# One encoder layer on one core: the read of y placed ahead of the stores, output weights split by ScalarE and VectorE, first weights of two groups side by side

## What is computed

```python
h = x @ w_in                                   # 7 parts of 512 columns: u_a, v_a, z_a, q, k, v_b, z_b
a_out = gelu(u_a) * (tril(w_s) @ layernorm(gelu(v_a)) + b_s)     # chunks of 128 frames, 4 channel groups
p = softmax(q @ k.T * HEAD_DIM_B ** -0.5 + bias)                 # own chunk of 64 frames and 8 before it, 8 heads
y = concat(a_out * silu(z_a), (p @ v_b) * silu(z_b))
out = layernorm(ALPHA * x + y @ w_out)
```

## Time and profile before

| | |
|---|---|
| median of three runs | 1073.99 us (1073.51 to 1074.5) |
| the profiled execution | 1073.99 us, of which the span is 1071.9 |
| busy: TensorE, weight loads | 1053.1 us (98%), 912.6 us (85%) |
| busy: VectorE, ScalarE, GpSimd | 459.8, 353.0, 157.2 us |
| chain that ended last | TensorE 97% |
| TensorE's clock over the span | 0.994 of full |

### The profile page before, as it was taken

One profiled execution on the slowest core, in us unless ns is written; L12 is line 12 of the kernel. 1 busy time (PEld: TensorE's weight loads), 2 busy tenths in 40 slices (PEclk: granted clock), 3 DMA queues, 4 the chain that ended last, 5 costly groups with the idle time before them and its releaser, 6 DMA issues.

```text
span 1071.9 us, 17673 instructions
## 1 busy us (share of the span) xinstructions
PE 1053.1 (98%) x7338; PEld 912.6 (85%) x7338; DVE 459.8 (43%) x944; ACT 353.0 (33%) x722; POOL 157.2 (15%) x160
## 2 busy tenths in 40 slices
PE   9999999999999999999999999999999999999995
PEld 7988889999999999999999887777888888888884
DVE  6545442212122111112112001877777777667654
ACT  6410011111111111111112112455666666666620
POOL 0011112020110000000000000742222222322211
PEclk9999999999999999999999999999999999999998
DMA  9561113222211233333331433765444543344112
GB/s 340 199 184 44 45 40 122 80 79 72 74 61 51 103 120 130 118 130 113 118 111 69 122 124 96 261 207 159 137 135 155 157 136 121 109 128 141 58 70 68
DMA packets 112287, 128.43 MB, mean 120 GB/s; under 512 B 7224, under 2 KB 86224, under 8 KB 112208
## 3 DMA queue, kind: packets, MB, share of 16 engines
q1 hardware_dynamic: 107312, 112.62, 32.6%
q10 hardware_dynamic: 4896, 14.68, 4.3%
HBM read 82.17 MB, written 48.26 MB: 122 GB/s over the span
## 4 chain that ended last, share of the span: by engine, by line
PE 97%; DVE 1%; DMA 1%; issue 0%; POOL 0%; POOLq 0%; ACT 0%; DVEq 0%; ACTq 0%; SPq 0%
PE s_ps L1228 35%; PE s_ps L1245 17%; PE out_ps L1430 16%; PE pt_ps L1228 8%; PE o_ps L1394 6%; PE s_ps L1323 6%; PE pt_ps L1365 3%; PE s_ps L1352 1%; PE s_ps L1430 1%; PE o_ps L1257 1%; PE out_ps L1257 1%; PE o_ps L1408 0%; PE out_ps L1264 0%; PE s_ps L1272 0%; DMA yr<-s_y 0%
## 5 line engine op out<-in xcount | busy, mean ns | idle before, releaser
L1228 PE MATMUL s_ps<-xh,ring 128*128 128x512 f32 (+1 forms) x1200 | 341.2, 362 | 0.8 <-ACT st L834 0.8
L1228 PEld LDWEIGHTS s_ps<-xh,ring 128*128 128x128 f32 x1200 | 221.2, 188 | 24.5 <-issue 1.2
L1228 PE MATMUL s_ps<-xl,ring 128*128 128x512 f32 (+1 forms) x600 | 217.1, 362 | 0.0
L1245 PE MATMUL s_ps<-ring,xh 128*128 128x512 f32 x544 | 169.8, 393 | 0.0
L1228 PEld LDWEIGHTS s_ps<-xl,ring 128*128 128x128 f32 x600 | 112.6, 188 | 11.9
L1245 PEld LDWEIGHTS s_ps<-ring,xh 128*128 128x128 f32 x544 | 100.5, 188 | 20.5 <-issue 0.3
L873 ACT ACTIVATE prob<-prob,low 128x640 f32<-128x640 f32 (+3 forms) x128 | 97.6, 764 | 57.5 <-DVE low L1078 57.5
L1078 DVE CUSTOM_DVE_ANT_1 prob<-s_ps,bias 128x640 f32<-128x640 f32 (+1 forms) x112 | 85.7, 803 | 54.5 <-PE s_ps L1323 54.3
L1430 PE MATMUL out_ps<-wo_h,yh 128*128 128x512 f32 x248 | 101.4, 409 | 4.8 <-DVE yl L1180 4.8
L1245 PE MATMUL s_ps<-ring,xl 128*128 128x512 f32 x272 | 106.0, 390 | 0.0
L1430 PE MATMUL out_ps<-wo_l,yh 128*128 128x512 f32 x248 | 98.3, 396 | 0.0
(11 more groups left out here) (151 smaller groups left out, 1225.1 us busy)
## 6 DMA issues: line engine op xcount, KB each, us to landing
raw<-w_all ACTq DMA_DIRECT2D x26, 512.0 KB, 3.6
r<-x SPq DMA_DIRECT2D x17, 512.0 KB, 3.8
q<-s_q SPq DMA_DIRECT2D x16, 512.0 KB, 4.2
k<-s_k SPq DMA_DIRECT2D x16, 512.0 KB, 6.0
y_out<-r SPq DMA_DIRECT2D x15, 512.0 KB, 2.7
x_raw<-x_t SPq DMA_DIRECT2D x12, 384.0 KB, 12.7
s_mix<-st SPq DMA_DIRECT2D x17, 256.0 KB, 2.3
v_all<-st SPq DMA_DIRECT2D x17, 256.0 KB, 2.0
```

The source lines that it names most:

```text
L1228: last = nc.tensor.matmul(bank[b][:, 0:width], w[:, kc, :], xx[:, kc, :], start=kc == 0 and a == 0, stop=kc == KC - 1 and a == 2)
L1245: last = nc.tensor.matmul(out, xx[:, kc, cols], ring[:, 0:GRP, side, kc, :], start=kc == 0 and a == 0, stop=kc == KC - 1 and a == 2)
```

## The change

It has three parts.

```diff
-PIECES = [(0, k0, k0 + 1) for k0 in range(KC)] + [(c, k0, k0 + 2) for c in range(1, NCH) for k0 in range(0, KC, 2)]
+PIECES = [(0, 0, 1, 0, 256), (0, 0, 1, 256, 512)] + [(0, k0, k0 + 1, 0, 512) for k0 in range(1, KC)]
+PIECES += [(c, k0, k0 + 2, 0, CHUNKS[c][1]) for c in range(1, NCH) for k0 in range(0, KC, 2)]
+Z_PIECES = [(0, 1), (1, 2), (2, 4), (4, 6), (6, 8)]
-IDLE_PRODUCTS = 9
+IDLE_PRODUCTS = 8
...
+WO_IN = {V_CYCLES - 1: [(0, 1), (2, 3)], V_CYCLES: [(4, 5), (6, 7)]}
...
+                for n in range(TILES):
+                    if START[n] - 2 == cycle:
...
+                        load_y(n)
                 for n in range(TILES):
                     if STORE[n] == cycle and n < TILES - 2:
...
                         load_values(b + 1)
-                for n in range(TILES):
-                    if START[n] - 2 == cycle:
...
-                        load_y(n)
...
-            for j in range(4):
-                split_wo(j)
             pool.wait_ge(proj_done, DONE["v", TILES - 1])
             nc.gpsimd.memset(qd[:], 0.0).then_inc(qd_zero, 1)
-            for j in range(4, 8):
-                split_wo(j)
...
-            for j in range(3):
-                for i in range(2):
-                    load_z_w(i, j)
-            for j in range(4):
-                for i in range(2):
-                    z_high(i, j)
-                    x_high(PIECES_OF[0][2 * j + i:2 * j + i + 1])
-                if j == 0:
-                    for i in range(2):
-                        load_z_w(i, 3)
+            load_z_w(0)
+            load_z_w(1)
+            act.wait_ge(const_ready, 2)
+            nc.scalar.activation(spare[:], eps[:], ACT.Copy)
+            load_z_w(2)
+            for j, (k0, k1) in enumerate(Z_PIECES):
+                z_high(j)
+                if j < 2:
+                    load_z_w(j + 3)
+                x_high([k + 1 for k in range(k0, k1)])
...
             for cycle in range(CYCLES):
                 copy_turned(2 * cycle - 2)
+                if cycle == V_CYCLES - 1:
+                    for j in (2, 3):
+                        high_wo(j)
                 for h in range(2):
                     exponent(2 * cycle, h)
+                if cycle == V_CYCLES:
+                    for j in (4, 5):
+                        high_wo(j)
...
                 copy_turned(2 * cycle - 1)
+                if cycle == V_CYCLES:
+                    for j in (6, 7):
+                        high_wo(j)
...
                     exponent(2 * cycle + 1, h)
+                if cycle == V_CYCLES - 2:
+                    for j in (0, 1):
+                        high_wo(j)
...
+            nc.vector.memset(st[3][:, 0:P], 1.0).then_inc(warm_ready, 1)
+            _, held = piece(0)
+            dve.wait_ge(x_loaded[0], 16)
+            nc.vector.tensor_copy(xh[0][held], x_raw[0][held]).then_inc(xh_first, 1)
+            for j, (k0, k1) in enumerate(Z_PIECES):
+                z_low(j)
+                x_low([0, 1] if j == 0 else [k + 1 for k in range(k0, k1)])
...
                         y_low_part(n)
+                if cycle in (V_CYCLES - 1, V_CYCLES):
+                    for j in WO_IN[cycle][0]:
+                        low_wo(j)
                 n, h = divmod(cycle - V_CYCLES, 2)
                 if n >= 0:
                     residual(n, h)
...
                             finish(n)
+                if cycle in (V_CYCLES - 1, V_CYCLES):
+                    for j in WO_IN[cycle][1]:
+                        low_wo(j)
...
-            pe.wait_ge(const_ready, 4)
+            pe.wait_ge(warm_ready, 1)
             for _ in range(IDLE_PRODUCTS):
-                nc.tensor.matmul(out_ps[:, 0:P], ident[:], ident[:], start=True, stop=True)
+                nc.tensor.matmul(out_ps[:, 0:P], st[3][:, 0:P], st[3][:, 0:P], start=True, stop=True)
...
-        "w_all": c(w_all),
+        "w_z": c(np.stack([w_all[0], w_all[1]], axis=2)), "w_all": c(w_all[2:]),
```

More of the change, by code:

```diff
@@ L46 @@
 V_FIRST = 24
[L49 removed]
+SLOT = [None, None, 0, 1, 2, 3, 4, 0, 1, 2, 3, 4, 0, 1, 2, 3, 4, 0, 1, 2, 0, 1, 3, 4, 0, 1, 2, 3]
 LOADED_BEFORE = [SLOT[2:i].count(s) for i, s in enumerate(SLOT)]
@@ L259, in hybrid_stream_step @@
         stats_v, mv_v, rstd_v = at("stats_v", here + 96, [6]), at("mv_v", here + 128, [2]), at("rstd_v", here + 160, [1])
-        here += 192
+        spare = at("spare", here + 192, [1])
+        here += 224
         slab = ctx.enter_context(nc.sbuf_tensor("slab", [P, (here + base - nc.sbuf_base) // 4], f32))
@@ L321, in hybrid_stream_step @@
         x_loaded = [sem(f"x_loaded{m}") for m in range(len(PIECES))]
+        warm_ready = sem("warm_ready")
         xh_done = sem("xh_done")
+        xh_first = sem("xh_first")
         x_split = sem("x_split")
-        z_w_loaded = [[sem(f"z_w_loaded{i}{j}") for j in range(4)] for i in range(2)]
+        z_w_loaded = [sem(f"z_w_loaded{j}") for j in range(len(Z_PIECES))]
         z_w_high = sem("z_w_high")
@@ L963, in x_low @@
                     c, held = piece(m)
-                    dve.wait_ge(xh_done, m + 1)
+                    if m:
+                        dve.wait_ge(xh_done, m)
+                    else:
+                        dve.wait_ge(xh_first, 1)
                     nc.vector.tensor_tensor(xl[c][held], x_raw[c][held], xh[c][held].bitcast(f32),
@@ L993, in chunk @@
                                                    op0=ALU.mult, op1=ALU.subtract).then_inc(evac[b], 1)
-            for j in range(4):
-                for i in range(2):
-                    z_low(i, j)
-                x_low(PIECES_OF[0][2 * j:2 * j + 2])
+            nc.vector.memset(st[3][:, 0:P], 1.0).then_inc(warm_ready, 1)
[5 more added lines that the diff above has]
+                x_low([0, 1] if j == 0 else [k + 1 for k in range(k0, k1)])
             x_low(PIECES_OF[1])
@@ L1259, in mix @@
                 last.then_inc(mix_done, 1)
-            pe.wait_ge(const_ready, 4)
+            pe.wait_ge(warm_ready, 1)
             for _ in range(IDLE_PRODUCTS):
-                nc.tensor.matmul(out_ps[:, 0:P], ident[:], ident[:], start=True, stop=True)
-            for kc in range(KC):
-                pe.wait_ge(xh_done, PIECES_OF[0][kc] + 1)
-                for i in range(2):
-                    if kc % 2 == 0:
-                        pe.wait_ge(z_w_high, kc + i + 1)
-                    nc.tensor.matmul(bank[i], w_high(i)[:, kc, :], xh[0][:, kc, :], start=kc == 0, stop=False)
-                    if kc % 2 == 0:
-                        pe.wait_ge(z_w_split, kc + i + 1)
-                    nc.tensor.matmul(bank[i], w_low(i)[:, kc, :], xh[0][:, kc, :], start=False, stop=False)
-                pe.wait_ge(x_split, PIECES_OF[0][kc] + 1)
+                nc.tensor.matmul(out_ps[:, 0:P], st[3][:, 0:P], st[3][:, 0:P], start=True, stop=True)
+            for m in PIECES_OF[0]:
+                _, kc, _, n0, n1 = PIECES[m]
+                if m:
+                    pe.wait_ge(xh_done, m)
+                else:
+                    pe.wait_ge(xh_first, 1)
+                split = [j for j, (k0, _) in enumerate(Z_PIECES) if k0 == kc]
+                for j in split:
+                    pe.wait_ge(z_w_high, j + 1)
+                for i in range(2):
+                    nc.tensor.matmul(bank[i][:, n0:n1], w_high(i)[:, kc, :], xh[0][:, kc, n0:n1], start=m == 0, stop=False)
+                for j in split:
+                    pe.wait_ge(z_w_split, j + 1)
                 for i in range(2):
-                    last = nc.tensor.matmul(bank[i], w_high(i)[:, kc, :], xl[0][:, kc, :], start=False, stop=kc == KC - 1)
+                    nc.tensor.matmul(bank[i][:, n0:n1], w_low(i)[:, kc, :], xh[0][:, kc, n0:n1], start=False, stop=False)
+                pe.wait_ge(x_split, m + 1)
+                for i in range(2):
+                    last = nc.tensor.matmul(bank[i][:, n0:n1], w_high(i)[:, kc, :], xl[0][:, kc, n0:n1], start=False, stop=kc == KC - 1)
                     if kc == KC - 1:
```

73 lines of the change are left out of this document (38 added, 35 removed).

## The result

The changed kernel takes **1063.97 us** (median of 4 runs, 1063.93 to 1064.1) against 1073.75 in the same session for the kernel before (1073.33 to 1074.5): a ratio of 0.9906 [0.9893, 0.9920], 9.8 us less where 11.4 were forecast. The span of the profiled execution is 1062.2 us instead of 1071.9, TensorE's mean granted clock 0.998.

A forecast was written before the change was run, and what follows sets the result against it. TensorE works almost throughout, so gains lie only where it idles or runs at its lower clock. End 7.1, middle 3.4 and opening 0.9 sum to 11.4 us: 1073.99 to 1062.6, range 1060.3 to 1066.

The forecast's parts named there:

- The end: Tile 16: reading y ahead of tile 14's store removes a 4.80 us wait and 2.34 of slow clock, 7.1 us.
- The edit in cycle 32 and in cycles 10 to 22: The same move of y's read at earlier tiles: later stores, reads and cached-value loads would cost nothing.
- The middle: Output weights' casts to ScalarE, subtractions to VectorE: 4.9 us gained less new waits of 1.2 and 0.3, 3.4 us.
- The new wait: Middle, before unit 8's scores: TensorE waits 1.2 us for VectorE's bias additions behind two output subtractions.
- the second, of 0.3: Middle, before unit 10's scores: TensorE waits 0.2 to 0.4 us for VectorE's unit 9 bias additions.
- (c): Rival, cycles 3 to 5: VectorE becomes the bound; subtractions at 1.8 us give 1067.2, at 2.39 give 1072.0; chance 0.06.
- (d): Rival, middle: VectorE's subtractions take 2.9 us or more, costing 13.4 us and giving 1076; chance 0.03.
- The 1.7 us of slow clock: Old middle, from 700.13: granted clock 0.54 over 3.74 us, counted as 1.7 us lost within the 4.9.
- The opening: First chunk: fewer unread products, earlier table load and smaller first x start real work sooner, 0.9 us, bounds -0.5 and 1.2.
- the cap: Opening: the second chunk's x transfers, with about 0.25 us from release to product, limit the gain to 1.2 us.
- rival (a): Opening gives nothing because weights of rows 256 on come late: 1063.5, to 1064.0 at the bound; chance 0.17.
- The longer rows: Opening: weights in 2 KB rows, not 1 KB, might double their transfer share, so rows 256 to 511 land near 7.

The follow-up runs named there:

- e2_end: The kernel before with only the read of y moved ahead of the stores: 1066.39 us, ratio 0.9931 to the kernel before.
- e1_end_middle: The kernel before with the read of y and the output weights changed, old opening kept: 1063.58 us, ratio 0.9905 to the kernel before.
- e9_opening: The kernel before with the new opening and nothing else: 1074.13 us, ratio 1.0009 to the kernel before.
- e4_x_whole: The changed kernel with the first row block's x in one load instead of two: 1063.06 us, ratio 0.9902 to the kernel before.
- e5_w_rows: The changed kernel with first x whole and first weights in eight loads of 1 KB rows: 1063.98 us, ratio 0.9902 to the kernel before.
- e10_two_waits: The changed kernel with the norm's gain and offset loaded earlier and VectorE's gating-bias copies moved later: ratio 0.9919 to the kernel before.
- e12_offset_early: The changed kernel with only the last norm's gain and offset loaded earlier: 1063.41 us, ratio 0.9898 to the kernel before.
- e8_all: The changed kernel with x whole, eight weight loads ahead, early output subtractions, early norm loads, later gating-bias copies: 1062.27 us, ratio 0.9884 to the kernel before.

## Why the prediction was right, and where not

**The end** was right in each step: the wait, the clock, the late store, the read of x in time. 7.14 us in the changed kernel, 7.3 in e2_end, forecast 7.1. The edit in cycle 32 and in cycles 10 to 22 shows no cost, as said.

**The middle** was right in mechanism, and in size in part by luck: 3.65 us against 3.4. The new wait came where it was put, 1.06 us instead of 1.2; the second, of 0.3, shows as no wait at all; a subtraction costs 1.22 us, so that rivals (c) and (d) fall. Two points behind the sum were not as I had them. The 1.7 us of slow clock were not worth 1.7: without the fall the old middle waits 0.90 us for GpSimd's subtraction and is only 0.54 us faster, so most of that loss lay over another. And measured against an execution whose clock did not fall, the same edit gains 2.8 to 3.1 (688.86 less 685.75 or, of e1_end_middle, 686.00), not 3.65. That the clock would not fall at the one new wait held: 1.00 behind 1.06 us. But two waits of 1.73 us together left it at 1.00 in e2_end, where 1.95 in the kernel before had brought it to 0.54, so the rows give no sharp rule. The Trainium skill, TensorE: Matmul & The Clock Gate, What's actually happening, says that the clock is set by how busy the PE has been recently; these executions don't test it.

**The opening** is the step that failed: "I take 0.9 us, nearer to the cap". It gave -0.54 by the trace, and nothing by e9_opening. The outcome is rival (a)'s, the cause isn't. I had weighed late weights for rows 256 to 511; what came late was x of the second row block, rows 128 to 255. The start itself came out better than forecast (first product at 4.54 instead of 5.15) and the first row block worse (0.64 us longer, where at most 0.5 was booked); without the wait of 1.45 the forecast would have been met. I had counted for the split of x only its six more products and VectorE's subtractions. Left out was the arrival of the next load: it has a later place in the queue (issued at 1.70 instead of near 1.2), and it takes longer from issue to landing (5.8 to 6.3 us with 2 KB rows, 4.2 to 4.9 in the old opening), while DMA moves less in the first 6 us. Why it moves less stays open. The longer rows that I had booked as a help for the weights helped nothing that a run shows. Late weights were there too, one step behind: with x in time they are what TensorE waits for (e4_x_whole). The cap of 1.2 us was not tested: it rests on 0.25 us from a release to the product, a figure that no run shows (in the openings the product follows 0.05 to 0.15 us behind the cast it waits for), and the best opening measured, e5_w_rows, is 0.65 better than that of the earlier trace rows and 1.2 better than the new one.

**The place not named** cost 0.52 us. In the middle I asked what is late next for y and for the output weights, and not for the queue as a whole: the sync queue did not get 3 us earlier when TensorE did, and the offset of the first norm is at its end. The table of nine executions shows it: the loss follows the offset's lateness, and it is absent where the offset is early (e10_two_waits, e12_offset_early).

Forecast less measured: 1.44 (opening) - 0.25 (middle) + 0.52 (offset) - 0.04 (end) = 1.67, and 11.4 - 1.67 = 9.73. The errors have both signs, so the total is nearer than its worst part.

## What to carry to other kernels

Work that runs beside TensorE is paid for only where TensorE waits, and then it is paid by what else it slows: taking two-input work from GpSimd freed VectorE's short operations. When a stage gets earlier, go through each queue that feeds it, to its end, and ask which transfer keeps its time; the next wait stands there. Splitting the first load to start sooner delays the next by a place in the queue, so work out when the second piece arrives as carefully as the first. And before a part below a microsecond is called a gain or a loss, look at it in more than one execution.

## What was not expected of the hardware

- In the new opening DMA has a low window of 0.6 us while loads are waiting: 111 to 190 GB/s from 3.60 us on with the first x in two loads, 149 to 202 from 4.80 on with it in one; the old opening has nothing below 260 from 3.0 to 6.0 us. The cause is open.
- In the opening products can run at about half their later pace (0.45 us, then 0.23, in e8_all) with a granted clock of 1.00 in the profile's rows. The column does not show the state in which a kernel starts; the pace of the products does. It differs from execution to execution of the same opening.
- The clock fell behind waits of 0.72 and 1.23 us and stayed up behind 0.50 and 1.23, and behind 0.43 and 1.23, at the same place.
